# The residual's norm from sums of x*z and z*z taken while a section ends, and x updated by accumulating DMAs

## The reference

```python
def _rmsnorm(x, g):
    y = x * lax.rsqrt(jnp.mean(x * x, axis=-1, keepdims=True) + EPS)
    return y * g
def _pre(x, g, mod, k):
    return _rmsnorm(x, g) * (1.0 + mod[:, 3 * k + 1][:, None]) + mod[:, 3 * k][:, None]
def _post(x, y, g, mod, k, weight):
    return x + weight * mod[:, 3 * k + 2][:, None] * _rmsnorm(y, g)
def _swiglu(h, w_gu, w_down):
    gate, up = jnp.split(h @ w_gu, 2, axis=-1)
    return (jax.nn.silu(gate) * up) @ w_down
```

## Time and profile before

| | us |
|---|---|
| median of 3 runs | 2658.51 |
| lowest, highest | 2654.53, 2658.70 |
| the profiled execution's own time | 2659.8 |
| its span in the profile | 2658.0 |
| TensorE busy | 2593.4 (98%) |
| VectorE busy | 1616.4 (61%) |
| GpSimd busy | 812.6 (31%) |
| ScalarE busy | 714.7 (27%) |

### The profile page before, as it was taken

One profiled execution on the slowest core, in us unless ns is written; L12 is line 12 of the kernel. 1 busy time (PEld: TensorE's weight loads), 2 busy tenths in 40 slices (PEclk: granted clock), 3 DMA queues, 4 the chain that ended last, 5 costly groups with the idle time before them and its releaser, 6 DMA issues.

```text
span 2658.0 us, 40824 instructions
## 1 busy us (share of the span) xinstructions
PE 2593.4 (98%) x17044; PEld 2436.5 (92%) x17044; DVE 1616.4 (61%) x2270; ACT 714.7 (27%) x1050; POOL 812.6 (31%) x1286
## 2 busy tenths in 40 slices
PE   6999999999999999999999999999999999999998
PEld 5999999998989899999999899999999878888886
DVE  6688878767574676676676633433434684544444
ACT  4222212123334411112212412112112424322222
POOL 1278876832140100000001248667551031000001
PEclk9999999999999999999999999999999999999999
DMA  9534544453464234434432422222223575233331
GB/s 336 153 124 157 157 143 134 159 181 124 124 193 143 81 95 134 135 111 130 133 105 86 112 68 82 94 96 87 93 96 125 175 195 159 72 96 95 95 95 64
DMA packets 340688, 334.55 MB, mean 126 GB/s; under 512 B 52496, under 2 KB 311704, under 8 KB 337432
## 3 DMA queue, kind: packets, MB, share of 16 engines
q1 hardware_dynamic: 278200, 198.19, 25.4%
q10 hardware_dynamic: 52288, 77.20, 8.7%
q0 software_dynamic: 10016, 56.56, 5.6%
HBM read 287.40 MB, written 44.50 MB: 125 GB/s over the span
## 4 chain that ended last, share of the span: by engine, by line
PE 84%; DVE 8%; DMA 2%; POOL 2%; issue 2%; ACT 1%; SPq 0%; DVEq 0%; POOLq 0%; ACTq 0%
PE ps L467 79%; POOL xT L1239 1%; DVE tmpN L1444 1%; DVE hL L1448 1%; DMA raw<-in_ffn_gu_dram 1%; PE ps L1259 1%; DMA adaW<-in_w_ada_dram 1%; ACT wH L452 1%; DVE zb L2075 1%; PE ps L1274 1%; DVE zd L2076 1%; PE ps L1004 1%; PE ps L1023 1%; DVE zc L2088 0%; DVE adaW L576 0%
## 5 line engine op out<-in xcount | busy, mean ns | idle before, releaser
L467 PE MATMUL ps<-hH,wH 128*128 128x384 f32 (+1 forms) x2928 | 1014.6, 347 | 8.8 <-DVE hL L1448 8.0
L467 PE MATMUL ps<-hH,wL 128*128 128x384 f32 (+1 forms) x2928 | 1005.5, 343 | 0.0
L467 PE MATMUL ps<-hL,wH 128*128 128x384 f32 (+1 forms) x2928 | 1005.4, 343 | 0.0
L459 DVE TENSOR_TENSOR wL<-raw,wH 128x1024 fp32r<-128x1024 f32 x300 | 389.5, 1310 | 477.0 <-ACT wH L452 475.5
L467 PEld LDWEIGHTS ps<-hH,wH 128*128 128x128 f32 x2928 | 550.5, 188 | 36.1 <-issue 7.4
L467 PEld LDWEIGHTS ps<-hH,wL 128*128 128x128 f32 x2928 | 550.6, 188 | 18.4
L467 PEld LDWEIGHTS ps<-hL,wH 128*128 128x128 f32 x2928 | 550.8, 188 | 18.0
L467 PE MATMUL ps<-midH,wH 128*128 128x384 f32 (+1 forms) x1232 | 424.8, 345 | 3.8 <-DVE yT L915 3.2
L452 ACT ACTIVATE wH<-raw 128x1024 fp32r<-128x1024 f32 x300 | 310.6, 1050 | 422.6 <-PE ps L467 407.4
L467 PE MATMUL ps<-midH,wL 128*128 128x384 f32 (+1 forms) x1232 | 422.2, 343 | 0.0
L467 PE MATMUL ps<-midL,wH 128*128 128x384 f32 (+1 forms) x1232 | 421.9, 342 | 0.0
(11 more groups left out here) (284 smaller groups left out, 2242.4 us busy)
## 6 DMA issues: line engine op xcount, KB each, us to landing
raw<-in_ffn_gu_dram SPq DMA_DIRECT2D x176, 512.0 KB, 3.9
adaW<-in_w_ada_dram ACTq DMA_DIRECT2D x40, 1536.0 KB, 7.1
raw<-in_ffn_down_dram SPq DMA_DIRECT2D x88, 512.0 KB, 3.5
x_d<-xT POOLq DMA_DIRECT2D x4, 3072.0 KB, 10.6
xT<-x_d POOLq DMA_DIRECT2D x4, 3072.0 KB, 11.3
ada_early<-in_w_ada_dram POOLq DMA_DIRECT2D x6, 1536.0 KB, 19.5
W_d<-gW POOLq DMA_DIRECT2D x16, 512.0 KB, 3.6
VT_d<-gVT ACTq DMA_DIRECT2D x16, 512.0 KB, 3.0
```

Of the source, the lines that this page charges most:

```text
L459: nc.vector.tensor_tensor(wL[:, n % SPLIT_SLOTS, :], raw[:, n % RAW_SLOTS, :], wH[:, n % SPLIT_SLOTS, :].bitcast(f32), ALU.subtract).then_ ...
L467: ins = nc.tensor.matmul(dst, a, b, start=first and n == 0, stop=last and n == 3 * len(pairs) - 1)
```

## The change

It touches how a section ends and what a joint does.

- The new x is x + r z, with z = coefP * y and r = 1/rms(y). Its sum of squares over the channels is sum x² + r (2 sum x z + r sum z²). The first term is kept from joint to joint (`sumX`). While a section's last eight chunks come, VectorE multiplies each y chunk by coefP and x (`cross_z`), ScalarE squares z (`square_z`), GpSimd adds those squares into sumZ beside sumY, and TensorE sums the products chunk by chunk between its own (`cross_sums`). `new_sums` puts the terms together on VectorE. Squares of x and their sums go, save at the very start.
- Chunk 0 is added to x by VectorE. Chunks 1 to 7 are added by DMAs with accumulation, issued by GpSimd as soon as a chunk of y is scaled, up to four under way. Chunks 3 to 7 of y are scaled inside `pre_vector`, one chunk ahead of their use, from a copy of the spread row that ScalarE makes (`rowY`).
- In the FFNs the last two down passes become one: four units of 256 columns over four inner chunks, so each of the last eight chunks is 24 matmuls, as in the mixer (`last_part`, `last_chunks`, `last_adds`).
- The late ada ride's steps all lie in the gate/up pair before, and TensorE takes its columns before chunk 2 of the last pass.
- A mixer begins with three units in `first_groups`; head_weights moves to banks 2 and 3 and its copy behind the first shift. A late split lies inside `pre_vector`.
- The last section's end adds x as before. At the start, unit 2's load waits for the fourth ada ride's load and its split comes later. The spill waits for all eight chunks of x.

```diff
+    def last_chunks(pe, S, moving, first):
...
+        for m in range(first, KC - 2):
+            pe.wait_ge(w_lo, S.wide + m // 2 + 1)
+            last_wait(pe, S, m)
+            signal(last_part(pe, S, m, moving, range(HC), (0, 1)), m)
+            while S.next and m >= 2 and summed < m:
+                cross_sums(pe, S, summed)
+                summed += 1
...
+    def last_adds(dve, S, ride=None):
...
+        for m in range(KC if S.tok0 else KC - 2):
+            last_ready(dve, S, m)
+            if ride is not None and m == LAST_RIDE_CHUNK:
+                take_columns_late(dve, ride, 2 * last_slot(S, m), TOK // 2)
+            at = sb_pair(yT[:, m, :], S.tok0)
+            nc.vector.tensor_tensor(at, ps_pair(last_slot(S, m), S.tok0), at, ALU.add).then_inc(S.read, 1)
+            if S.next:
+                dve.wait_ge(S.read, S.read0 + m + 1)
+                cross_z(dve, S, m, token_segments(S.tok0), True)
+            if m % 2 and m < KC - 1:
+                split_lo(dve, S.wide + 3 + m // 2)
...
+    def add_squares(pool, N, S):
+
+        for m in range(1, KC - 2):
+            for tile, squares_of, ready, done in ((sumY, lambda c: sq[:, c], sq_y, sum_y),
+                                                  (sumZ, lambda c: squared(S, c), sq_z, sum_z))[:2 if S.next else 1]:
+                pool.wait_ge(ready, KC * N.nth + m + 1)
+                ins = nc.gpsimd.tensor_tensor(tile[:, N.tok0:TOK], (squares_of(0) if m == 1 else tile)[:, N.tok0:TOK],
+                                              squares_of(m)[:, N.tok0:TOK], ALU.add)
...
+        for m in range(1, KC):
             pool.wait_ge(y_norm, KC * N.nth + m + 1)
-            add_to_x(pool, nc.gpsimd, N, m, x_new_pool)
+            if m > 4:
+                wait_x(pool, N, m - 4)
+            pool.dma_start(xT[:, m, N.tok0:TOK], yT[:, m, N.tok0:TOK], accum_op=ALU.add).then_inc(x_added[m % 4], 16)
...
+    def square_z(act, S, m, segments, done):
+
+        for t0, t1, v in segments:
+            ins = nc.scalar.activation(squared(S, m)[:, t0:t1], yT[:, m, t0:t1], ACT.Square, scale=coefP[:, m, v:v + 1])
...
+    def cross_z(dve, S, m, segments, done):
+
+        for t0, t1, v in segments:
+            ins = nc.vector.scalar_tensor_tensor(crossed(S, m)[:, t0:t1], yT[:, m, t0:t1], coefP[:, m, v:v + 1],
+                                                 xT[:, m, t0:t1], ALU.mult, ALU.mult)
...
+        dve.wait_ge(ss_z, N.nth + 1)
+        columns(dve, bank + 1, N.tok0, sumD).then_inc(cols_z, 1)
+        dve.wait_ge(rs_y, N.nth + 1)
+        dve.wait_ge(cols_z, N.nth + 1)
+        dlink(dve, nc.vector.tensor_tensor(d, d, r, ALU.mult))
+        dve.wait_ge(ss_x, N.nth + 2)
+        columns(dve, 7, N.tok0, cross).then_inc(cols_x, 1)
+        dve.wait_ge(cols_x, N.nth + 2)
+        dsync(dve)
+        dlink(dve, nc.vector.scalar_tensor_tensor(d, c, 2.0, d, ALU.mult, ALU.add))
...
-    def pre_vector(dve, N):
...
+    def pre_vector(dve, N, late=()):
...
         for m in range(first, KC):
...
+            if post and m + 1 < KC and m + 1 >= AHEAD_Y:
+                scale_y(dve, post, m + 1)
             if m >= 2:
                 dve.wait_ge(h_lo, KC * N.nth + m - 1)
+            new_chunk(m)
             for t0, t1, v in token_segments(N.tok0):
                 ins = scaled(m, t0, t1, v)
             ins.then_inc(h_tmp, 1)
             if m >= 1:
                 rest(m - 1)
...
-                    flip_rows(dve, nxt)
+                    if N.tok0 == 0:
+                        dve.wait_ge(bc_y_ctx, N.ctx_nth + 1)
+                    dsync(dve)
+                    scale_y(dve, N, 0)
                     inverse_x(dve, nxt)
-                    for n in S.late[1:]:
-                        split_lo(dve, n)
-                    pre_vector(dve, nxt)
+                    dve.wait_ge(y_norm, KC * N.nth + 1)
+                    add_to_x(dve, nc.vector, N, 0, x_new)
+                    dve.wait_ge(row_y, N.nth + 1)
+                    for m in range(1, 3):
+                        scale_y(dve, N, m)
+                    pre_vector(dve, nxt, S.late)
```

More of the change, by code:

```diff
@@ L266, in build @@
     x_new = sem("x_new")
-    x_new_pool = sem("x_new_pool")
+    x_last = sem("x_last")
+    x_added = [sem(f"x_added{m}") for m in range(4)]
     sq_x = sem("sq_x")
@@ L375, in make_pre @@
         N.layer, N.k, N.tok0, N.sq = layer, k, tok0, sq
-        N.banks = (4, 5) if k == 1 else (6, 7)
+        N.banks = (6, 7)
         return N
@@ L410, in build @@
         p[1].next = p[3]
+        p[2].has_next = p[3] is not None
         pre.after = N
@@ L866, in ffn_scalar @@
         load_root(act)
-        for m in range(KC if N.tok0 else KC - 2):
-            square_y(act, N, F, m)
-        if N.tok0 == 0:
-            square_last(act, N, F)
+        squares(act, N, F)
     def ffn_vector(dve, F):
@@ L908, in down @@
                     dve.wait_ge(w_used, F.base + i + 2)
-                if last is not None and m == LAST_RIDE_CHUNK:
-                    take_columns_late(dve, last, 2 * tile_slot(F, g + m), TOK // 2)
                 if p == 0:
@@ L954, in build @@
-    HALF = TOK // 2
+            if s < NPH - 2:
+                down(8 + 6 * s, 8 + 12 * s, s, ride_at(F, s + 1, 0) if more else None,
+                     ride_at(F, s + 1, 1) if more else None)
+        last = F.ride0 + FFN_RIDES - 1 if F.ride0 is not None and F.late_rides else None
+        dve.wait_ge(down_read, F.n0["down_read"] + KC * (NPH - 2))
+        last_adds(dve, F, last)
+    HALF = TOK // 2
+    def last_adds(dve, S, ride=None):
+        coef_post(dve, S.post)
+        if S.next:
+            coef_pre(dve, S.next)
+            wait_back(dve, S.post)
+        dsync(dve)
[5 more added lines that the diff above has]
+            nc.vector.tensor_tensor(at, ps_pair(last_slot(S, m), S.tok0), at, ALU.add).then_inc(S.read, 1)
+            if S.next:
+                dve.wait_ge(S.read, S.read0 + m + 1)
+                cross_z(dve, S, m, token_segments(S.tok0), True)
+            if m % 2 and m < KC - 1:
+                split_lo(dve, S.wide + 3 + m // 2)
+        if S.tok0 == 0:
+            for m in (KC - 2, KC - 1):
+                add_first_half(dve, S, m, last_slot(S, m))
+                dve.wait_ge(half_read, 2 * S.post.nth + m - (KC - 2) + 1)
+                cross_z(dve, S, m, part_segments(0, 0), False)
+            for m in (KC - 2, KC - 1):
+                last_ready(dve, S, m)
+                add_second_half(dve, m, last_slot(S, m), S.read)
+                dve.wait_ge(S.read, S.read0 + m + 1)
+                cross_z(dve, S, m, part_segments(0, 1), True)
@@ L1437, in build, with late_parts @@
     LATE_COEFS = {4: (5, 7), 7: (6, 8)}
-    def pre_vector(dve, N):
-        dve.wait_ge(bc_x if N.tok0 else bc_x_ctx, (N.nth if N.tok0 else N.ctx_nth) + 1)
+    def pre_vector(dve, N, late=()):
+        post = N.after
+        if N.tok0 == 0:
+            dve.wait_ge(bc_x_ctx, N.nth + 1)
+        else:
+            dve.wait_ge(bc_x, N.nth + 1)
         dsync(dve)
+        AHEAD_Y = 3
+        def late_parts():
+            for n in late:
+                split_lo(dve, n)
         def scaled(m, t0, t1, v):
@@ L2021, in mix_scalar @@
         load_root(act)
-        for m in range(KC if tok0 else KC - 2):
-            square_y(act, N, M, m)
-            if m % 2 and m < KC - 1:
-                split_hi(act, M.base + 17 + m // 2)
-        if tok0 == 0:
-            square_last(act, N, M)
+        squares(act, N, M)
     def by_chunk(t, m, tok0):
@@ L2357, in start_vector @@
                 inverse_x(dve, pres[0])
-        for n in range(SPLIT_SLOTS):
+        for n in range(2):
             split_lo(dve, n)
```

473 lines of the change are left out of this document (268 added, 205 removed).

## The result

The changed kernel takes 2695.8 us (median of 4 runs, 2689.6 to 2697.2) against 2656.9 for the kernel before in the same runs: 1.44% slower, ratio 1.0144, interval 1.0131 to 1.0157. The forecast was slower, 2676, range 2650 to 2702. The direction and the range held, but the loss is 39 us where 18 were reckoned, more than twice as much.

The account below looks back on a forecast made before the run. TensorE, busy 98% of the span, was taken as the bound. FFN joints +7.4, mixers +10.4 and joint 5 +5.2 gave +23.0, less 4.9: +18, 2678 against 2659.8, about 2676 as a median; range 2650 to 2702.

Parts of the forecast that it names:

- A joint is read at the third unit, not at the first product: After a joint, time counts where TensorE is no longer fed chunk by chunk: T+47.5 in joint 3, T+35.5 in joint 5.
- L: In the joints, time from a scale's end to x ready through an accumulating DMA: 4.2 us, 3.5 on 512 tokens.
- What L costs: Every second chunk of a joint waits, four pairs: hL(7) 2.8 us later, in joint 5 4 x 1.35.
- The ledger for a joint with nothing late: VectorE's steps after T, DMAs hidden: first product T+13.5, hL(7) T+37.0, against T+37.8 now; joint 5 T+26.2.
- the spill behind them, which moves from before to after the first product, [is] hidden: Spill of x in the joints: costs nothing; uncovered, it and two other items cost up to 1 us a joint.
- 10.9 us from unit 0 to usable inputs: Mixer entry: from unit 0's end through copy, store and loads to usable state inputs, taken as 10.9 us.
- The clock: TensorE's granted clock falls to half after the joint: some 2 us each, slow side, folded into the range; no chance given.
- VectorE against GpSimd: Before T, crosses and GpSimd's additions hardly overlap: last chunks' sums and crosses 1.7 us late, 2.4 on 512 tokens.
- rival E: VectorE loses every meeting with GpSimd's ten additions: start at T+19 instead of 15.2, +19 on the forecast, 2695; chance 0.08.
- The removed waits, -4.9: TensorE's waits of 1.5 and 2.5 us in the first two FFNs and 0.9 at the end go: -4.9 us.
- Rival D: Loss before T and L = 6 us (5 on 512 tokens) in the joints: +50, 2708; chance 0.07.

Follow-up runs that it names:

- the tiny spill: The changed kernel with the two mixers' spills of x cut to 16 columns; 2685.0 us, ratio 1.0106.
- the run with the ride alone: The kernel before with all sixteen steps of the late ada ride in the gate/up pair ahead, none in the down pass; 2654.0 us, ratio 0.9985.

## Why the prediction was right in sign and wrong in size

- *A joint is read at the third unit, not at the first product.* Right. The first product came 8.5 us earlier in joint 1 and the kernel lost. The three units ended at T+48.8 and T+48.9 in joints 2 and 3, forecast 48.9; joint 5 at T+37.0, forecast 38.9.
- *L = 4.2 us, from the plain write plus a second read.* Right: 4.27, of which 3.9 are the landing, 3.3 for 256 KB. The Trainium skill's figure for one DMA and its two source reads for an add ("DMA: Bandwidth & Descriptors", Anatomy of one DMA, and "Collectives: The Full Stack", Why ReduceScatter is half of AllGather) gave 3.8 as an estimate. The landing measured 3.9, and 3.3 where the same estimate gives 3.2, so the trace agrees.
- *What L costs.* Too small, the second term that failed. The sum had 4 x 2.8 + 5.4, about 17 us; covering the DMA gave back 30. Part of it is the shorter iteration, 3.17 us where the ledger had 3.5; part is products at the lower clock behind the gaps; and part came back in the mixers, whose first turn moved from T+76.4 to T+72.6 and, in joint 4, from T+75.7 to T+69.6. The ledger for a joint with nothing late was too dear at the same time (hL(7) at T+34.1 to 37.4 with everything else unchanged, forecast 38.7), which is why the sum of a too small L and a too long ledger met the FFN joints so closely.
- *"the spill behind them, which moves from before to after the first product, [is] hidden".* This is the step that failed. The prediction put the spill at nothing, with 1 us a joint as the most that it and two other items could cost, and gave no reason but the engine's free queue; it did not ask what the spill would run beside. Its 3 MB now go out while the mixer's first quarter is stored, and that store is on the chain that the mixer waits for. The prediction took 10.9 us from unit 0 to usable inputs as a constant; the store in it went from 3.1 to 6.5 us. In the changed kernel this costs about 10 us (the tiny spill), of the 17 by which the mixers missed their forecast; on the kernel before, where the store starts earlier in the spill, it costs 23.
- *The clock.* Named as a rival and folded into the range at 2 us a joint. It did fall, in every joint and in the state inputs (5.08 against 2.79 us). Filling the gaps put most of it right without a measurable gain, so its own price stays unsettled.
- *VectorE against GpSimd.* Right in kind and about in size: 1.7 us per joint forecast for the start (2.4 in joint 5), 2.4, 0.7, 2.4, 3.7 and 0.0 us measured, 6 us in all against 9. VectorE does not lose every meeting: 3.37 against 1.15 for a cross, but also 2.83 against 1.84 for an addition, and rival E with its 19 us did not come. That is the rule of the Trainium skill, "SBUF — State Buffer", Who interferes with whom: whoever issues first has the shared port pair for the whole instruction. The trace agrees: the two halves of the cross at 871.21 end at 872.30 and 874.58, just behind the ends of GpSimd's additions at 872.01 and 874.03.
- *The removed waits, -4.9.* The 2.5 in f20 went and took 1.6 at the lower clock along (4.1 us by the run with the ride alone). The 1.5 in f10 gains nothing by the ride alone. In the changed kernel f10's T did not move although it has five cross sums of 0.46 us more; TensorE's waits between 560 and T fell from 2.2 to 0.6 us, which gives back most of these 2.3. The 0.9 us at the very end, credited as removed for sure, is still there: TensorE now waits them for ScalarE's square.
- *The rest.* In f11, 1.2 us are a wait of TensorE for a cross inside the section (from 2053.2) that the prediction had at nothing; 0.8 are unexplained. In the mixers the traces divide the miss. Against the forecast's inputs 3 us later than before, the first turn came 9.8 and 9.5 us later. Of these 6.8 and 6.5 us too much the spill explains 5.9 and 4.3, and 0.9 and 2.2 are left, where unit 0 comes late (its copy starts at T+43.9 and 45.0, the sum had 42.6) and the state inputs are at the lower clock. Behind the first turn the miss is 1.5 and 2.3 us; 1.7 of the latter are the longer stretch at the lower clock (13.7 us against 10.2), the other 2.1 are unexplained.
- *Rival D* was added up too low: with its own terms an FFN joint costs 10.9 and a mixer 12.4 us, not 10 and 11.6, and its time is about 2711. The range's upper end, between E and D, still holds 2702.

## What to carry to other kernels

When a transfer that nobody waits for is moved, ask what it now runs beside, not only who reads it: a 3 MB spill that had landed 26 us before the first step that may not begin without it cost 10 us, and 23 in the kernel before, because a 384 KB store on the path stood beside it. A step handed to a DMA must be covered for its whole latency from the producer's end (4.3 us here for 384 KB), and one more stage of lookahead, a change of four lines, was worth 30 us. A difference between two traces is only worth what it is at the same clock: 5 us of one mixer came and went with a stretch that no change touched. And read a joint where the next section is no longer fed piece by piece: the first product came 8.5 us earlier and the kernel became slower.

## What the runs showed of the hardware

A DMA that accumulates 384 KB from on-chip memory into on-chip memory, issued by GpSimd, lands in 3.9 us (median), 256 KB in 3.3, against 2.9 for a plain write of 384 KB to memory; two issued together in joint 1 took 4.9 and 6.0, and beside chunks of a spill the last four there took 5.2 to 5.6. A 384 KB store issued 3 us into a 3072 KB write on another queue takes 11.6 us, issued 7.6 us into it 6.5 us, and alone 2.3 to 3.1: it landed 0.2 and 2.4 us behind the large one. VectorE's instructions with two on-chip operands and GpSimd's additions held each other up in both directions (3.37 against 1.15 us, 2.83 against 1.84). TensorE's granted clock stood at its lower level behind gaps of 3.1 and 7.1 us (0.50 and 0.55).
